# A decoder layer on eight cores: the first norm table built on chip, attention's score and V Wo products reordered, transposes spread over four banks

## What is computed

```python
def reference(x, mem, ...):
    mem_n = rmsnorm(mem, mem_norm_g)
    x = x + rmsnorm(parallel_conv_mixer(rmsnorm(x, mix_pre_g), ...), mix_post_g)
    x = x + rmsnorm(memory_cross_attention(rmsnorm(x, xa_pre_g), mem_n, w_q, w_k, w_v, w_o), xa_post_g)
    x = x + rmsnorm(swiglu_ffn(rmsnorm(x, ffn_pre_g), w_gate, w_up, w_down), ffn_post_g)
    return x
```

## Time and profile before

| | us |
|---|---|
| median of 3 runs | 889.1 (887.85 to 889.79) |
| the profiled execution, its own time | 889.61 |
| span of its slowest core, core 7, first to last instruction | 887.0 |
| spans of the eight cores | 884.3 to 887.0 |
| core 7: PE idle before its instructions, 0 to 26 us | 20.4 |

### The profile page before, as it was taken

How to read it: one execution, slowest core, us unless ns; L and a number is a source line. 1 busy time by engine, 2 the same in 40 slices (tenths; PEclk the granted TensorE clock), 3 DMA queues, 4 the chain that set the end, 5 groups by cost and what they waited for, 6 DMA issues and landing times.

```text
span 886.4 us, 13126 instructions; the slowest of 8 cores (884.3 to 887.0 us)
## 1 busy us (share of the span) xinstructions
PE 849.1 (96%) x4795; PEld 432.8 (49%) x4872; DVE 390.0 (44%) x500; ACT 298.3 (34%) x544; POOL 125.9 (14%) x290
## 2 busy tenths in 40 slices
PE   2899999999999899999999999999999999999997
PEld 1657444555664455554444444444444444444443
DVE  1477758437547678886522122331232322221122
ACT  2332345532636668765331111221122211111111
POOL 3121113112103132321110010000000000000000
PEclk9999999999999999999999999999999999999999
DMA  9599057368894257877696012122121121210011
GB/s 195 153 179 192 1 185 253 124 128 139 168 221 91 50 148 188 190 153 184 194 182 118 1 72 95 37 60 72 72 95 36 48 84 72 67 53 1 1 48 71
DMA packets 33327, 97.94 MB, mean 110 GB/s; under 512 B 11344, under 2 KB 11472, under 8 KB 32368
## 3 DMA queue, kind: packets, MB, share of 16 engines
q0 software_dynamic: 7344, 33.03, 23.4%
q1 hardware_dynamic: 25920, 64.07, 21.5%
HBM read 107.05 MB, written 20.97 MB: 144 GB/s over the span
## 4 chain that ended last, share of the span: by engine, by line
PE 92%; ACT 3%; issue 2%; DMA 1%; DVE 1%; DVEq 0%; SPq 0%; POOL 0%; POOLq 0%; ACTq 0%
PE pp L374 89%; PE pp L433 3%; ACT t L354 3%; DMA t<-x 1%; DVE t L1003 1%; DVE t L367 0%; ACT L354 0%; DVEq L1193 0%; SPq L377 0%; DVE t L371 0%; POOLq L1193 0%; ACT pp L354 0%; POOL t L357 0%; ACTq L187 0%; POOL t L363 0%
## 5 line engine op out<-in xcount | busy, mean ns | idle before, releaser
L374 PE MATMUL pp<-t,t 128*128 128x512 bf16 (+2 forms) x4195 | 819.2, 354 | 7.9 <-ACT t L354 2.7
L374 PEld LDWEIGHTS pp<-t,t 128*128 128x128 bf16 x4272 | 397.0, 98 | 411.2 <-issue 6.9
L357 DVE TENSOR_TENSOR t<-pp,t 128x512 bf16<-128x512 f32 (+4 forms) x173 | 150.4, 873 | 365.8 <-PE pp L374 194.7
L354 ACT ACTIVATE t<-pp 128x512 f32<-128x512 f32 (+5 forms) x208 | 153.3, 750 | 355.8 <-PE pp L374 336.6
L367 DVE SCALAR_TENSOR_TENSOR t<-t,t,t 128x1024 bf16<-128x1024 f32 (+4 forms) x100 | 126.5, 1271 | 49.3 <-POOL t L357 29.7
L361 POOL TENSOR_SCALAR t<-t 128x1 f32<-128x1 f32 (+2 forms) x102 | 24.7, 242 | 627.5 <-ACT t L354 323.3
L433 PE MATMUL pp<-t,t 128*128 128x128 bf16 (+1 forms) x600 | 43.2, 222 | 23.0 <-DVE t L367 19.8
L354 ACT ACTIVATE pp<-pp 128x1024 f32<-128x1024 f32 (+1 forms) x17 | 16.3, 958 | 142.4 <-PE pp L374 142.4
L357 POOL TENSOR_TENSOR t<-t,t 128x1 f32<-128x1 f32 (+2 forms) x103 | 60.7, 589 | 15.6 <-POOL t L361 0.6
L354 ACT ACTIVATE t<-pp,t 128x256 bf16<-128x256 f32 (+2 forms) x76 | 43.9, 583 | 42.8 <-DVE t L1003 34.2
L354 ACT ACTIVATE t<-t 128x1024 bf16<-128x1024 f32 (+2 forms) x52 | 53.9, 1037 | 8.7 <-DMA t<-x 8.7
(11 more groups left out here) (26 smaller groups left out, 65.2 us busy)
## 6 DMA issues: line engine op xcount, KB each, us to landing
t<-x SPq DMA_DIRECT2D x68, 512.0 KB, 6.7
x<-t SPq DMA_DIRECT2D x24, 512.0 KB, 3.6
t<-w_gu POOLq DMA_DIRECT2D x22, 512.0 KB, 6.8
out<-t SPq DMA_DIRECT2D x15, 512.0 KB, 2.8
t<-w_dn POOLq DMA_DIRECT2D x6, 768.0 KB, 20.2
t<-gains SPq DMA_DIRECT2D x6, 512.0 KB, 9.4
t<-w_ing POOLq DMA_DIRECT2D x8, 256.0 KB, 16.5
t<-w_inc POOLq DMA_DIRECT2D x4, 512.0 KB, 10.4
```

Of the source, the lines that this page charges most:

```text
L354: S.op("act", lambda e: e.activation(out=out, in_=in_, func=func, **kw), reads, writes)
L357: S.op(eng, lambda e: e.tensor_tensor(out=out, in0=in0, in1=in1, op=op), reads, writes)
L374: S.op("pe", lambda e: e.matmul(out, lhsT=lhsT, rhs=rhs, start=start, stop=stop), reads, writes, signal)
```

## The change

Four things change; no product of the reference is left out.

1. **The G0 load goes.** SP now issues the identity first, then the gain as 8 rows of 128 values (`g_row`, 4 KB), then block 0 of x and the others. DVE makes `gsel`, eight selectors of 8x128 out of the identity (one broadcast copy), and splits each gain value into three bfloat16 pieces (`gain_rows`: three casts and two subtractions on 8x128). PE adds them up on 128 partitions with 24 matmuls of 128 columns (`gain_bcast`). The norm of block 0 reads the table straight from PSUM; an ACT copy writes it to G0 for the others.
2. **The start-up calls are written in another order.** `glu_part` gets hooks, by which a transpose stands between two units, and `pre_ev`, calls that are recorded ahead of the eviction. The first part holds the unit (0,0) alone, ahead of the transposes of block 1.
3. **z_t** takes the banks of groups 2 and 3 from `pair()`.
4. **Attention.** No part of B is made ahead of the loop. Part 0 stands behind the scores of block 0, parts 1 to 4 behind its exponentials (part 2 in `pp[0]`), parts 5 and 6 behind the scores of block 1, part 7 behind the transposes `t_p(0)` and `t_a(3)`. The scores of blocks 0 and 1 use the same pair. For i = 0 and 1 the square `pre_a(i + 3)` stands behind the exponentials.

```diff
+        grow = buf([8, 2, 128], F32, U0 + 36864, ["grow0", "grow1"])
+        gpc = buf([8, 3, 128], BF16, U0 + 37888, ["gpc0", "gpc1", "gpc2"])
+        gsel = buf([8, 8, 128], BF16, U0 + 38912, ["gsel"])
...
-                stt(hs, xap, r, g[0:n, :], MUL, MUL, [xkey, "st%d" % i, gkey], ["hs%d" % s])
+                stt(hs, xap, r, g[0:n, :], MUL, MUL, [xkey, "st%d" % i] + (gkey if isinstance(gkey, list) else [gkey]),
+                    ["hs%d" % s])
...
+        def gain_rows():
+            for p in range(3):
+                cp("dve", gpc[:, p, :], grow[:, p % 2, :], ["grow%d" % (p % 2)], ["gpc%d" % p])
+                if p < 2:
+                    tt("dve", grow[:, 1 - p, :], grow[:, p, :], gpc[:, p, :], SUB, ["grow%d" % p, "gpc%d" % p],
+                       ["grow%d" % (1 - p)])
+
+        def gain_bcast():
+            pt, bk = pair()
+            for kc in range(8):
+                for p in range(3):
+                    mm(pt[:, kc * 128:(kc + 1) * 128], gsel[:, kc, :], gpc[:, p, :], p == 0, p == 2,
+                       ["gsel", "gpc%d" % p], [bk[kc // 4]], p == 2 and kc % 4 == 3)
+            return pt, bk
...
         xset[0] = [0, 1, 2, 3, 4, 9, 12, 13]
-        xs0 = {0: load_x(x_d[0])}
         idf = ev[:, 0, 0:128]
         dma("sp", "ident", idf, id_d, [], ["ev0"])
-        dma("sp", "G0", G0[:], gain_d[GN_MIXPRE], [], ["G0"])
+        dma("sp", "grow", grow[:, 0, :], grow_d, [], ["grow0"])
+        xs0 = {0: load_x(x_d[0])}
         for b in range(1, 8):
             xs0[b] = load_x(x_d[b], ["x%d" % xs0[b - 2]] if b >= 3 else [])
...
         cp("dve", ident[:], idf, ["ev0"], ["ident"])
+        cp("dve", gsel[:, :, :], ident[0:8, 0:8].unsqueeze(2).broadcast_to([8, 8, 128]), ["ident"], ["gsel"])
+        gain_rows()
...
-        def glu_part(units):
+        def glu_part(units, hooks={}, pre_ev=None):
             pt, bk = pair()
             for u, (b, c) in enumerate(units):
+                if u in hooks:
+                    hooks[u]()
...
+            if pre_ev is not None:
+                pre_ev()
             glu_evict(pt, bk, [(u0, u1, zst[:, c0 * 8:c1 * 8, b, :], "zs%d" % b) for u0, u1, b, c0, c1 in runs],
                       len(units))()
...
         def z_t(t):
             for q in range(4):
-                pv, bk = tbank()
+                if q < 2:
+                    pv, bk = tbank()
+                else:
+                    if q == 2:
+                        zpt, zbk = pair()
+                    pv, bk = zpt[:, (q - 2) * 512:(q - 1) * 512].bitcast(BF16), zbk[q - 2]
                 for gg in range(8):
...
+        def tq(b, eng):
+            return lambda: t_x(b, hp[b], eng)
         q1(0)
-        q2(0)
+        gpt, gbk = gain_bcast()
+        hp[0] = prep2(pt1[0], xt[xs0[0]], "x%d" % xs0[0], gpt, gbk)
         t_x(0, hp[0], "dve")
         q1(1)
+        act(G0[:, :], gpt[:, :], AF.Copy, gbk + ["hs%d" % hp[0]], ["G0"])
         q2(1)
-        t_x(1, hp[1], "dve")
         q1(2)
-        glu_part([(0, 0), (1, 0)])
-        q2(2)
-        t_x(2, hp[2], "dve")
+        glu_part([(0, 0)], pre_ev=lambda: (t_x(1, hp[1], "dve"), q2(2)))
         q1(3)
-        q2(3)
-        glu_part([(0, 1), (1, 1), (2, 0), (2, 1)])
+        glu_part([(1, 0), (0, 1), (1, 1)], {1: tq(2, "dve")}, lambda: q2(3))
         q1(4)
-        t_x(3, hp[3], "dve")
-        q2(4)
-        glu_part([(0, 2), (1, 2), (3, 0), (3, 1)])
+        glu_part([(2, 0), (2, 1), (0, 2), (1, 2)], {2: tq(3, "dve")}, lambda: q2(4))
         q1(5)
-        t_x(4, hp[4], "act")
-        q2(5)
-        glu_part([(2, 2), (3, 2), (4, 0), (4, 1)])
+        glu_part([(2, 2), (3, 0), (3, 1), (3, 2)], {1: tq(4, "act")}, lambda: q2(5))
         q1(6)
-        t_x(5, hp[5], "act")
-        q2(6)
+        glu_part([(4, 0), (4, 1), (4, 2)], {2: tq(5, "act")}, lambda: q2(6))
         wload_c(0)
         glu_part([(0, 3), (1, 3), (2, 3), (3, 3)])
         q1(7)
         q2(7)
         wload_c(1)
-        glu_part([(4, 2), (4, 3), (5, 0), (5, 1)])
         t_x(6, hp[6], "act")
         hx = prep(tm0[0:HALO, :], "tm0", G0, "G0", HALO)
+        glu_part([(4, 3), (5, 0), (5, 1)])
         glu_part([(5, 2), (5, 3)])
         t_x(7, hp[7], "act")
...
-        def b_mm(r0, r1):
-            for rc in range(r0, r1):
-                pt, bk = pair()
+        def b_mm(rc, i, eng):
+            if True:
+                pt, bk = pp[i], ["bk%d" % (2 * i), "bk%d" % (2 * i + 1)]
...
-                if rc % 2 == 0:
-                    act(Bm[:, rc, :], pt[:, :], AF.Copy, bk, ["B%d" % rc])
-                else:
-                    cp("dve", Bm[:, rc, :], pt[:, :], bk, ["B%d" % rc])
-
-        b_mm(0, 6)
+                copy_on(eng, Bm[:, rc, :], pt[:, :], bk, ["B%d" % rc])
...
             if i >= 3:
                 po[i - 3][1]()
             if i < NB:
+                p0 = 1 + rrp[0] % 3
+                p1, p2 = 1 + p0 % 3, 1 + (p0 + 1) % 3
                 sc_mm(i)
                 sc_max(i)
-            if i + 3 < NB:
+            if i == 0:
+                b_mm(0, p1, "act")
+            if i == 1:
+                b_mm(5, p1, "act")
+                b_mm(6, p2, "act")
+            if i + 3 < NB and i > 1:
                 pre_a(i + 3)
             if i < NB:
                 sc_exp(i)
-            if i == 1:
-                b_mm(6, 8)
+            if i == 0:
+                b_mm(1, p2, "dve")
+                b_mm(2, 0, "dve")
+                b_mm(3, p1, "act")
+                b_mm(4, p2, "dve")
+                rrp[0] -= 1
+            if i < 2:
+                pre_a(i + 3)
             if i == NB:
                 for k in range(2):
                     ffn_slice(0, GORD[k], sgx[k][:, :], "sgx%d" % k)
@@ -1097,6 +1132,9 @@
                 t_p(i - 1)
             if i + 2 < NB:
                 t_a(i + 2)
+            if i == 1:
+                b_mm(7, p1, "dve")
+                rrp[0] += 1
...
-        "cb": c_(np.broadcast_to(f(conv_b_b)[None, :], (128, 512))),
+        "g_row": c_(f(mix_pre_g).reshape(8, 128)), "cb": c_(np.broadcast_to(f(conv_b_b)[None, :], (128, 512))),
```

1 line of the change is left out of this document (added).

## The result

The changed kernel takes **882.99 us** (882.3 to 883.9) where the kernel before takes 888.97 beside it: a ratio of 0.9936, with a 95% interval of 0.9925 to 0.9948. The forecast was 877.2, with a range of 872.8 to 881.6. The direction was right. Of the 11.9 us in the sum, 6.0 came, and the time lies 1.4 us outside the range.

What follows compares the result with a forecast made beforehand. PE, 92% of the chain, was taken as the bound. Start-up 7.2, z_t 1.6 and attention 3.1 sum to 11.9 us off the 887.0 span: 875.1, plus 2.6 outside gives 877.7, median 877.2 us, range 872.8 to 881.6.

Steps and rivals of the forecast that it cites:

- the sum: Whole kernel: 7.2 us at start-up, 1.6 in z_t and 3.1 in attention make a gain of 11.9 us.
- What bounds the kernel: PE makes 92% of the chain, so only stretches where it idles or runs slowly can give time.
- start-up: First stretch on PE: gain of 7.2 us from earlier transposes, clock and hooks, bounds 5 and 9.5.
- Block 0 at 6.1 us: Start-up loads: without G0, block 0 goes out 0.9 us later than before and lands at 6.1 us.
- Rival 1: Start-up: late weights, or blocks gaining at most half the forecast move, leave 4.2 us, 880.2 in all; chance 0.15.
- The table: Start-up: the gains' table stands in PSUM at about 9.0 us, hidden by block 0's root up to 9.8.
- The units' order: Start-up on PE: unit (0,0) waits for wg1, starts at 15.0; block 2's transposes start 5.6 us earlier, at 20.3.
- z_t: Transposes in z_t: groups 2 and 3 stop waiting for copies, gain 1.6 us, bounds 1.0 and 2.0.
- Attention: Start of the attention loop: gain 3.6 less a 0.5 us wait of t_p(1), 3.1 us, bounds 1.5 and 3.7.
- Rival 2: Attention: ACT's late exponentials stall scores of blocks 1 and 2, gain falls to about 0.5, 879.8; chance 0.12.
- the clock at start-up: PE at start-up: the clock level rises at 24.1 us, losing 1.9 instead of 2.8 us, gain 0.9.
- The weights' issues and the shared side: Start-up on POOL: DVE casts could hold back the last weight issues by the skill's rule; one trace pair showed no lengthening.

Runs made afterwards that it cites:

- the best version: The changed kernel with block 0's load first on SP's queue and part 4's square back ahead of block 1's exponentials: 878.15 us, ratio 0.9863.

## Why the prediction was off, step by step

**What bounds the kernel** was read rightly: all the gain there was lay in the start-up row, in z_t and at the start of attention.

**Block 0 at 6.1 us: wrong, and it cost some 2 us** (1.6 in the mean of the cores). The step was "Without G0 each later block moves into the place ahead of it: block 0 goes out 0.9 us later and lands at 6.1". It took a landing as an issue time plus a fixed length. In the earlier trace rows, block 0's 4.1 us were measured with block 0 at the head of the queue and before the weights' packets had come. The rows of the kernel before did not show what a late place costs. Its bound should have been the cost of sharing that the same rows do show, where block 1, queued behind others with the weights beside it, takes 12.7 us. Block 0 landed 3.1 us later than forecast (9.2), and its norm, not wg1, set the first unit.

The same step was wrong for the blocks behind. In the mean of the cores block 1 landed at 12.6 (forecast 11.1 to 11.8; 14.5 before), block 2 at 16.6 (15.2; 18.2 before) and block 3 at 21.8 (19). That is about half of the move that the sum gave to blocks 1 and 2. Rival 1 had this as its second condition, with a chance of 0.15, 4.2 us for start-up and 880.2 for the whole. Start-up gave 4.6 in the mean of the cores and 5.1 on the slowest, so its size was about right. It came by another way, though: block 0, which the rival did not name, held the first unit, and the weights of its first condition held none.

**The table: right.** Identity on DVE at 3.12 (3.4), selector copy 0.68 (1.0), table at 8.4 (9.0), hidden. It is hidden only while block 0 is late, though: with block 0 first, the table ended at 10.7 to 12.3, and it binds.

**The units' order: right in kind.** On core 5 of the changed kernel no wait stands between units behind 24 us. Where PE comes there earlier, or block 3 later, one of up to 1.9 us stands ahead of block 3's transposes (0.79 on core 5 of the best version), because block 3 was not there at 19. The first unit with block 0 in front came at 14.4 to 16.0. That this is the forecast 15.0 is luck: there the prediction had the unit wait for wg1, and the runs have it wait for the table; wg1 was there by 14.4. With both repairs, start-up is worth 7.9 us on the slowest core and 6.5 in the mean; the sum had 7.2.

**z_t: right.** The term was 1.6 and the runs have 2.0, the upper bound; the cause was that the drain at each wait goes as well, as I had counted at start-up and not here. The new 0.3 to 0.4 at the first output projection was not seen.

**Attention: wrong at one instruction.** The step was "The normalisation of block 1 ends at 303.9, so t_p(1) waits about 0.5". Everything up to it held. Moved by the 6.8 us that this stretch began earlier, the exponentials of block 1 were to end at 295.2 and ended at 295.05; PE was to be free at 296.7 and was at 296.8. But from the exponentials I went straight to the normalisation, and did not walk DVE's own list. It had `sca_a(4)` between the two, and the change had moved that cast's input (square, POOL) behind the exponentials. In the prediction's terms, the 0.5 us that it set against the gain of 3.6 was the term that was too small. The wait was 3.15 us, 2.6 more than forecast. Rival 2 was of this kind, with a gain of 0.5, which is what was measured up to t_p(1); but it named ACT as the late engine, and the place was DVE.

**The clock behind the wait: not considered.** The prediction weighed the clock at start-up alone. A wait of 3.15 us inside a busy row took up to 2.9 us more, on seven of eight cores.

**The whole.** The best version's ratio of 0.9863 is 12.2 us at 889; the sum was 11.9. Its parts agree too: start-up 6.5 to 7.9 for 7.2, z_t 2.0 less 0.3 for 1.6, attention 2.4 for 3.1 (27.1 us before, 24.7 now), with a wait of 1.26 left where 0.5 was forecast. The opportunity was sized rightly, in part by luck (the first unit, and the clock on core 5); the changed kernel takes half of it.

**The weights' issues and the shared side.** POOL's eight `w_ing` issues on core 5 of the changed kernel, and on the same core with block 0 first:

```profile
1.55 4.92 POOL L381 DMA_DIRECT2D t<-w_ing  x8 [0.86 <-POOLq L202]
```

```profile
1.55 4.48 POOL L381 DMA_DIRECT2D t<-w_ing  x8 [0.86 <-POOLq L202]
```

In the kernel before they take 4.48 or 4.49 us on all eight cores; in the changed kernel 4.66 to 4.92 on all eight, with 2.2 us of DVE casts, copy and subtractions between 3.1 and 5.8. With block 0 first (the run of that move alone), DVE's work on core 5 begins at 6.1, when the issues are out, and they take 4.48 again. In the best version the identity is in use at 4.77 on core 1 and 5.12 on core 5, and the issues take 4.60 and 4.71 there, 4.48 or 4.49 on the other six. With the weights behind block 0 the two are apart as well, and it is 4.48 or 4.49. The prediction had one pair of rows and concluded that nothing is lengthened; the lengthening is real and small, 0.1 to 0.4 us. The Trainium skill (SBUF — State Buffer, "SBUF: two separate sides") says that DVE and GpSimd hold the pair of ports that they share one at a time, for a whole instruction. By that rule the runs agree in direction, and show that here the lock costs a fifth of DVE's busy time in the changed kernel (0.44 of 2.2 us on core 5), and a quarter on core 5 of the best version (0.23 of 0.9).

## What to carry to other kernels

When an instruction is moved, walk every engine's list past the ones that consume what it makes: an in-order engine that waits for the moved result holds back all that stands behind it, ready or not. At the start of a kernel, being first on the queue is itself the thing of worth; a landing time read with a load at the head does not hold two places further back. And look at the cores' spread: a wait in the middle of a dense TensorE row costs its length on every core and the lower clock on some, and the slowest core is the time.
